# Latent attention in a hybrid trunk: scores from rounded and low parts, outputs by key tile

## The reference, cut to what matters

```python
q = (c_q @ w_uq).reshape(B, L, H, 192)            # 128 + 64 rotary
kv = (c_kv @ w_ukv).reshape(B, L, H, 128 + 128)   # keys, values
k = concatenate([kv[..., :128], k_pe shared by the heads])
q, k = rms_norm(q, g_q), rms_norm(k, g_k)         # then rotary on the last 64
s = einsum("bqhd,bkhd->bhqk", q, k) * scale       # where(mask, s, NEG_INF)
o = einsum("bhqk,bkhd->bqhd", softmax(s), v)
y = o.reshape(B, L, H * 128) @ w_o
```

## Time and profile before

| | us |
|---|---|
| median of 3 runs | 2914.8 |
| the three runs | 2919.31, 2914.8, 2913.06 |
| span of the profiled execution (PE busy 96% of it) | 2919.8 |
| the profiled execution's own time: highest of the runs, beside its span | 2919.31 |
| PE busy, of the span | 2817.5 |
| DVE, ACT, POOL busy | 1800.3, 926.7, 670.6 |
| mean granted clock of PE, as a share of 2.4 GHz | 0.983 |

### The profile page before, as it was taken

One profiled execution on the slowest core, in us unless ns is written; L12 is line 12 of the kernel. 1 busy time (PEld: TensorE's weight loads), 2 busy tenths in 40 slices (PEclk: granted clock), 3 DMA queues, 4 the chain that ended last, 5 costly groups with the idle time before them and its releaser, 6 DMA issues. The chain is left out here.

```text
span 2919.8 us, 57859 instructions
## 1 busy us (share of the span) xinstructions
PE 2817.5 (96%) x23164; PEld 2700.8 (93%) x23164; DVE 1800.3 (62%) x2735; ACT 926.7 (32%) x1407; POOL 670.6 (23%) x327
## 2 busy tenths in 40 slices
PE   8999999999999999999878999999999999999999
PEld 7788999998888899999768999999999999899987
DVE  5443677713777687778796687741354535787730
ACT  4443322222444232222264322222222223332221
POOL 2111100043322220003532400024433334200033
PEclk9998999999999999999889999999999999999999
DMA  3100222232211122232300222233322122122232
GB/s 131 44 23 30 80 93 88 99 101 92 66 61 58 36 95 88 92 95 86 104 2 24 95 80 93 91 104 101 108 79 95 61 91 75 44 94 92 87 115 80
DMA packets 65558, 231.53 MB, mean 79 GB/s; under 512 B 8048, under 2 KB 8816, under 8 KB 64912
## 3 DMA queue, kind: packets, MB, share of 16 engines
q1 hardware_dynamic: 62784, 222.56, 23.3%
q10 hardware_dynamic: 2640, 7.02, 0.7%
HBM read 227.45 MB, written 2.10 MB: 79 GB/s over the span
## 5 line engine op out<-in xcount | busy, mean ns | idle before, releaser
L238 PE MATMUL ps<-xs,wr 128*128 128x264 f32 x12864 | 1577.4, 284 | 17.5 <-POOL wr L216 9.9
L238 PEld LDWEIGHTS ps<-xs,wr 128*128 128x128 f32 x12864 | 1561.9, 188 | 24.2 <-POOL wr L216 9.9
L216 POOL TENSOR_TENSOR wr<-raw,wr 128x1024 fp32r<-128x1024 f32 x240 | 588.6, 2458 | 2073.3 <-ACT wr L208 2072.7
L238 PE MATMUL ps<-hid,wr 128*128 128x264 f32 x5376 | 657.6, 284 | 10.4 <-POOL wr L216 6.0
L238 PEld LDWEIGHTS ps<-hid,wr 128*128 128x128 f32 x5376 | 653.7, 189 | 12.5 <-POOL wr L216 6.6
L208 ACT ACTIVATE wr<-raw 128x1024 fp32r<-128x1024 f32 x416 | 434.2, 1048 | 345.8 <-PE ps L238 264.9
L466 DVE TENSOR_TENSOR ub<-ps,rstd 128x528 f32<-128x528 f32 x176 | 124.4, 707 | 145.7 <-PE ps L238 145.0
L216 DVE TENSOR_TENSOR wr<-raw,wr 128x1024 fp32r<-128x1024 f32 x176 | 214.2, 1217 | 0.0
L526 ACT ACTIVATE hid<-scr 128x528 f32 x88 | 56.8, 646 | 382.2 <-DVE scr L485 382.2
L523 ACT ACTIVATE scr<-scr 128x528 f32<-128x528 f32 x88 | 56.9, 646 | 368.1 <-DVE scr L481 368.1
L478 DVE SCALAR_TENSOR_TENSOR scr<-ub,convp,scr 128x528 f32<-128x528 f32 x176 | 135.3, 769 | 26.0 <-DVE scr L475 21.1
(11 more groups left out here) (295 smaller groups left out, 2328.0 us busy)
## 6 DMA issues: line engine op xcount, KB each, us to landing
raw<-in_stream SPq DMA_DIRECT2D x416, 512.0 KB, 3.7
work<-in_ret_tab ACTq DMA_DIRECT2D x4, 1056.0 KB, 5.3
h<-in_h SPq DMA_DIRECT2D x8, 264.0 KB, 6.4
out<-h SPq DMA_DIRECT2D x8, 256.0 KB, 4.3
work<-in_s_b ACTq DMA_DIRECT2D x1, 512.0 KB, 3.5
work<-in_s_c ACTq DMA_DIRECT2D x1, 512.0 KB, 5.4
convp<-in_convp ACTq DMA_DIRECT2D x4, 88.0 KB, 2.3
work<-in_mla_tab ACTq DMA_DIRECT2D x1, 264.0 KB, 2.6
```

The source lines that it names most:

```text
L216: pool.tensor_tensor(wr[:, s, 1].rearrange("p a b -> p (a b)"), raw[:, s, :], wr[:, s, 0].rearrange("p a b -> p (a b)").bitcast(F32), ALU. ...
L238: mm = pe.matmul(out[:, q], wr[:, slot, w, b0 + k], x[k][v][:, q * HALF:(q + 1) * HALF], start=start and k == 0 and p == 0, stop=stop and ...
```

## The change

Scores: `qn, qr, kn, kr` are each split into a rounded part (ACT, `part_high`) and a low part (DVE, `part_low`) in fp32r, one set for all heads, and a score tile is the sum of three products for each of the two key parts (high by high, high by low, low by high). The 528 keys of block 3 go as 264 and 264, in two banks, and the mask is one fp32r matmul of 64 columns per block. Outputs: instead of one for each query block, `output` runs once for each head, in the next head's cycle where O3 was, over all 512 queries: the meta values by 512 columns, then key tile t by the queries from block t on (512, 384, 256, 128 columns), still in fp32. For that `pt` holds all transposed blocks, and the meta keys are transposed first. The last head's outputs are made in two parts, OA (blocks 0 to 2) and OB (block 3). ACT's and DVE's splits of the outputs go from four of 128 columns to one of 512. The diff, without the semaphore lists and the tables of waits that go with it (the waits for outputs now name O, OA or OB), and without the SBUF addresses:

```diff
-            CYCLE = (("S0", 0), ("S1", 0), ("O3", -1), ("S2", 0), ("SPK", 1), ("SPQ", 1), ("T0", 0), ("S3", 0), ("kn", 2), ("qn", 2),
-                     ("qr", 2), ("T1", 0), ("O0", 0), ("T2", 0), ("O1", 0), ("O2", 0), ("SUM", 2), ("T3", 0))
+            CYCLE = (("S0", 0), ("S1", 0), ("O", -1), ("S2", 0), ("SPK", 1), ("SPQ", 1), ("T0", 0), ("S3", 0), ("kn", 2), ("qn", 2),
+                     ("qr", 2), ("T1", 0), ("T2", 0), ("SUM", 2), ("T3", 0))
...
+            FINAL = (("S0", 0), ("S1", 0), ("O", -1), ("S2", 0), ("T0", 0), ("S3", 0), ("T1", 0), ("T2", 0), ("TM", 0),
+                     ("OA", 0), ("OM", 0), ("out0", 0), ("T3", 0), ("out1", 0), ("OB", 0))
...
+                def products(out, q, k, stop):
+                    for s, t in (("qn", "kn"), ("qr", "kr")):
+                        for v, w in PRODUCTS:
+                            pe.matmul(out, parts[s][v][:, q], parts[t][w][:, k], start=s == "qn" and (v, w) == PRODUCTS[0],
+                                      stop=stop and s == "qr" and (v, w) == PRODUCTS[2])
...
                     if b == 0:
-                        pe.wait_ge(p_scaled.sem, p_scaled.done("qr", h))
-                        pe.matmul(f[0:META, K:K + META], qn[j][:, 0:META], kn[j][:, 0:META], start=True, stop=False)
-                        pe.matmul(f[0:META, K:K + META], qr[j][:, 0:META], kr[j][:, 0:META], start=False, stop=True)
-                    for c0, c1 in ((0, min(K, 512)), (512, K)):
-                        if c0 < c1:
-                            pe.matmul(f[:, c0:c1], qn[j][:, q0:q0 + P], kn[j][:, c0:c1], start=True, stop=False)
-                            pe.matmul(f[:, c0:c1], qr[j][:, q0:q0 + P], kr[j][:, c0:c1], start=False, stop=False)
-                    for c0, c1 in ((K - 64, min(K, 512)), (512, K)):
-                        if c0 < c1:
-                            mm = pe.matmul(f[:, c0:c1], hide, ones[0:1, 0:c1 - c0], start=False, stop=True)
+                        pe.wait_ge(p_lo.sem, p_lo.done("qr", h))
+                        products(f[0:META, K:K + META], slice(0, META), slice(0, META), True)
+                    s = scored(b, h)
+                    for c0, c1 in ((0, K),) if b < QB - 1 else ((0, HALF), (HALF, K)):
+                        products(s[:, c0:c1], slice(q0, q0 + P), slice(c0, c1), c1 < K)
+                    mm = pe.matmul(s[:, K - 64:K], hide, every[0:1, 0:64], start=False, stop=True)
                     mm.then_inc(a_pe.sem, a_pe.one(f"S{b}"))
...
+                def output(name, h, b0, b1):
+                    o = o_pe if name == "O" else e_pe
+                    free(name, h)
+                    f = line(name, h)
+                    pe.wait_ge(a_act.sem, a_act.done(f"copy{b1 - 1}", h))
                     d = slice(h * VDIM, (h + 1) * VDIM)
+                    pe.matmul(f[:, b0 * P:b1 * P], vt[0:META, QB, d], pt[0:META, 0, b0 * P:b1 * P], start=True, stop=False)
+                    for t in range(b1):
+                        q = slice(max(t, b0) * P, b1 * P)
+                        mm = pe.matmul(f[:, q], vt[:, t, d], pt[:, t + 1, q], start=False, stop=t == b1 - 1)
+                    mm.then_inc(o.sem, o.one(name))
...
+                def part_low(s, h):
+                    dve.wait_ge(p_hi.sem, p_hi.done(s, h))
+                    dve.tensor_tensor(parts[s][1], whole(s, h), parts[s][0].bitcast(F32), ALU.subtract)\
+                       .then_inc(p_lo.sem, p_lo.one(s))
...
                 mean_squares(1)
+                for s in ("kn", "kr", "qn", "qr"):
+                    part_low(s, 0)
                 for h in range(HEADS):
...
-                    low(0, h)
                     share(3, h)
+                    if not last:
+                        for s in ("kn", "kr", "qn", "qr"):
+                            part_low(s, h + 1)
                     if h + 2 < HEADS:
                         rot(h + 2)
...
+                def part_high(s, h):
+                    act.wait_ge(p_scaled.sem, p_scaled.done(s, h))
+                    if h and s == "kn":
+                        act.wait_ge(a_pe.sem, a_pe.done("S3", h - 1))
+                    one(p_hi, s, parts[s][0], whole(s, h), ACT.Copy)
...
                     rotary(h)
+                    if h == 1:
+                        for s in ("kn", "kr", "qn", "qr"):
+                            part_high(s, 0)
                     roots(h)
...
                     soft(3, h)
+                    if not last:
+                        for s in ("kn", "kr", "qn", "qr"):
+                            part_high(s, h + 1)
                     if more:
                         query(h + 2)
                         round_unit(act, uH + h + 2 + AHEAD)
                         rotary(h + 2)
                     copy(1, h)
-                    high_out(0, h)
                     copy(2, h)
```

More of the change, by code:

```diff
@@ L151, in trunk @@
         convp = sb("convp", [P, 2 * KT, 4])
+        every = sb("every", [P, 192], F32R)
         work_at = hid_at + 8 * 2 * T * 4
@@ L570, in mla @@
             flat_work = work[:].rearrange("p a b -> p (a b)")
-            parity = lambda k: [work[:, 4 * j + k] for j in range(2)]
-            qn, qr, kn, kr = (parity(k) for k in range(4))
+            parts = {s: [parts_[:, 2 * k + v] for v in range(2)] for k, s in enumerate(("qn", "qr", "kn", "kr"))}
             krot, sqkr, tab, misc = (work[:, k] for k in (8, 9, 10, 11))
@@ L578, in mla @@
             par, stat, joint = misc[:, 0:16], misc[:, 16:56], misc[:, 56:57]
-            hide = misc[0:1, 64:192]
+            hide = every[0:1, 64:192]
+            hidden = -2.0 ** 100
             small, total, inverse = misc[0:META, 192:200], misc[0:META, 200:208], misc[0:META, 208:216]
@@ L651, in mla @@
             NEW = ["x", "a", "b"]
-            l_dve = Order(sem("mla_l_dve"), ["hide", "show"] + [("kv", s) for s in NEW] + [("kv", "root")] + ["joint", "tab"] +
+            l_dve = Order(sem("mla_l_dve"), ["every", "hide", "show"] + [("kv", s) for s in NEW] + [("kv", "root")] + ["joint", "tab"] +
                           [("norm", 3), ("norm", 4), ("lo", 3), ("lo", 4)] + ["gain", "up", "down", "turned", "twice"] +
@@ L897, in last_cycle @@
                     out_part(1, h, range(HEADS - 1))
-                    output(3, h)
-                    pe.wait_ge(a_dve3.sem, a_dve3.done("lo3", h))
+                    output("OB", h, QB - 1, QB)
+                    pe.wait_ge(e_dve.sem, e_dve.done("OB"))
                     out_part(0, h, [HEADS - 1])
@@ L952, in dve_ @@
             def dve_(dve):
-                dve.memset(hide[:, 0:64], NEG).then_inc(l_dve.sem, l_dve.one("hide"))
-                dve.memset(hide[:, 64:P], 0.0).then_inc(l_dve.sem, l_dve.one("show"))
+                dve.memset(every[0:1, 0:64].bitcast(F32), 1.0).then_inc(l_dve.sem, l_dve.one("every"))
+                dve.memset(hide[:, 0:64].bitcast(F32), hidden).then_inc(l_dve.sem, l_dve.one("hide"))
+                dve.memset(hide[:, 64:P].bitcast(F32), 0.0).then_inc(l_dve.sem, l_dve.one("show"))
                 norm_dve(dve, n, g0)
@@ L1113, in dve_ @@
                     if h:
-                        low(3, h - 1)
+                        low("O", h - 1, 0, QB)
                     if not last:
@@ L1136, in dve_ @@
                         mean_squares(h + 2)
-                low(3, HEADS - 1)
-                dve.wait_ge(a_dve3.sem, a_dve3.done("lo3", HEADS - 1))
+                low("OB", HEADS - 1, QB - 1, QB)
+                dve.wait_ge(e_dve.sem, e_dve.done("OB"))
                 dve.sem_inc(tile_free, gO - gV)
```

121 lines of the change are left out of this document (55 added, 66 removed).

## The result

The changed kernel takes 2926.5 us (median of 20 runs, 2913.2 to 2929.8 without one run of 5502.6), the kernel before 2917.3 (20 runs, 2912.0 to 2924.4). The ratio is 1.002, with a 95% interval of 1.001 to 1.0029: slower by 0.1 to 0.3%. The profiled executions have spans of 2927.5 and 2919.8 us and mean granted clocks of 0.976 and 0.983. The forecast was 2921, 6.2 above the median of the three runs shown with it. The size was about right, and so was the kind of reason. Both halves of the sum were too small, as the stage shows.

What follows compares the result with a forecast made beforehand. PE, busy 96% of the span, was taken as the bound. Terms summed to -4.4 us at full clock and +6 for lower clock, +1.6 on the profiled 2919.8, so 2921.4; 2921 was chosen, range 2901 to 2930.

Steps and rivals of the forecast that it cites:

- Both halves of the sum: Whole kernel: -4.4 us at the full clock and +6 us from lower clock, together +1.6.
- The case called likeliest: Whole kernel: time as summed, 2921 us, own range 2915 to 2927; chance 0.5.
- the middle head: Heads 1 to 5: 22.9 us becomes 20.1 without waits, 21.7 with PE's 1.6 us wait.
- Scores: PE's score products S0 to S3: 7.3 us a head becomes 5.85, 1.5 less.
- The count by passes: Score tiles: three passes for four save a quarter of product time, some 0.25 us a head beyond the sum.
- Outputs: PE's output products: 4.46 us a head becomes 3.2, 1.3 less.
- ACT's queue: Four copies behind S3's exponential end ACT's chain at 8.4 us; PE, there at 6.8, waits 1.6.
- The clock: Half speed after idle stretches at the start (+5 us) and in heads 6 and 7 (+1): +6 us.
- fourth rival: Waits at the sums of squares cost clock in middle heads too: six stretches of 3.4 us, +10, 2931 us; chance 0.1.
- no stretch with PE idle for 3 us keeps the clock: Trace of the kernel before: no 3 us idle PE stretch keeps the clock; argued against the clock doing as before.
- The second: Rival for the whole kernel: clock does as before, -4.4 from the median, 2910 us (2907 to 2914); chance 0.23.
- The third: Rival: ACT's chain ends by PE's arrival, heads 0 to 5 gain another 1.6 us each; 2896 to 2906; chance 0.17.

Runs made afterwards that it cites:

- experiment 5: Changed kernel with 13 overwritten 512-column products filling PE's idle time ahead of head 0's first scores only: 2920.8 us, ratio 1.0015 to the kernel before.
- experiment 6: Changed kernel with ACT's rounding of a weight unit moved behind the square of the rotary part: 2910.3 us in one run.
- experiment 7: Changed kernel with the four rounding copies ahead of the key's operations and remaining PE waits filled with unread products: 2898.8 us, ratio 0.9935 to before.
- experiment 2: Kernel before with only the new outputs by key tile, scores left as they were: 2909.6 us, ratio 0.9963 to before.
- experiment 4: Changed kernel with ACT's four rounding copies ahead of the key's operations and DVE's subtractions ahead of the last share: 2911.7 us, ratio 0.9968 to before.
- experiment 10: Changed kernel with three more unread ACT copies of 264 columns among the part copies of heads 1 to 7: 2945.6 us, ratio 1.008 to before.
- experiment 3: Changed kernel with unread 512-column products in PE's waits at the start, sums of squares, T3 of head 6, S0 of head 7: 2912.4 us, ratio 0.9963.
- experiment 12: Kernel with early copies and filled waits, with the exponential of S3 moved ahead of the key's operations on ACT: 2899.3 us, ratio 0.9937 to before.
- experiment 11: Changed kernel with the idle time ahead of the first scores filled by 28 products of 128 columns: 2923.7 us, ratio 1.0017 to before.
- experiment 9: Kernel with early copies and filled waits, with two of four part copies moved back behind the exponential of S3: 2902.7 us, ratio 0.9949 to before.
- experiment 8: Kernel before with only the outputs changed, plus unread products filling PE's waits in heads 6 and 7: 2903.5 us, ratio 0.9955 to before.

## Why the prediction was right, and where not

**The total** came out 9.2 us above before in the medians (2926.5 against 2917.3) and 7.7 in the profiled spans, inside the range. The case called likeliest happened: a small gain in PE's work, and a larger loss to the clock. But the gain was put at 4.4 us and the clock at 6, and neither is right: they were 7.0 and 14.7. Like for like, profile against profile, the sum said +1.6 and the stage gave +7.7. The 2921 came out closer because it was chosen between the median of three runs and a profile 5 us above it, and because the two errors go against each other. That much of it is luck.

**At the full clock** the stage gained 7.0 us, not 4.4. First what half speed cost, as each window less that of the same head at the full clock: head 0 22.65 - 18.10 (experiment 5) = 4.6, head 3 25.97 - 21.23 = 4.7, head 5 0.2, head 6 21.12 - 16.57 (212.84 to 229.41 in experiment 6) = 4.6, head 7 40.37 - 30.33 (experiment 7) = 10.0, together 24.1. For before an estimate must do: one us at half speed cost 0.46 us in head 3 (4.74 in 10.4), so 20.5 cost 9.4. The difference is 14.7; the stage ended 7.7 later, so the rest is -7.0. By heads: the start +2.5 (first scores at 91.04 instead of 88.55; forecast +2.8); head 0 -3.2 (18.10 against 21.29, 88.55 to 109.84 before; forecast -2.9); heads 1 to 5 5 x (21.23 - 22.87) = -8.2 (forecast -6.0); head 6 +0.5 (16.57 against 18.26 - 0.46 x 4.7; forecast +0.7); head 7 +1.5 (30.33 against 37.68 - 1.56 - 7.3 = 28.8, its window in rows 1 ending 1.56 us after the last product starts; forecast +1.0). That adds to -6.9. The term that was mis-sized is the middle head: forecast 21.7, measured 21.23.

**Scores.** Forecast 1.35, 1.19, 1.53 and 1.78 us. The timeline gives 1.26, 1.08, 1.49 and 1.84, 5.67 instead of 5.85. S0 and S1 were 0.1 shorter each; the 0.2 us for one exposed load and drain was perhaps too much behind narrow records, but no run separates it. S0 got no faster than the 1.24 of before: the narrowest tile gains nothing, while S1 went from 1.48 to 1.08. The count by passes that the prediction took from the Trainium skill (FP8 and Floating Point Precision, TensorE Precision Notes) would have made S0's products a quarter shorter; S0 took 1.24 us before and 1.26 after, and the trace decides against it.

**Outputs.** Forecast 3.2 us, measured 3.21. The gain of 1.3 a head is confirmed by itself in experiment 2 (22.87 to 21.54 or 21.57).

**ACT's queue.** Forecast, counted from the first projection: key product at 1.78, copies from 3.65 to 5.9, the end of the square at 8.4, PE at the sums at 6.8, a wait of 1.6. Measured with the projection at 124.62: 1.76, 3.53 to 5.66, 8.3, 6.87, and 1.47. Experiment 6 takes one term out of this queue and gets its full length back, experiment 4 takes four out and the wait is gone, experiment 10 puts three in and the wait grows by 0.95. This step is shown. What the prediction did not ask is whether the copies could stand elsewhere: ACT was idle for 2.94 us right ahead of them.

**DVE** was forecast to be done with its subtractions 7.3 us after the first projection; they ended 6.8 after it, hidden as said.

**The clock** is the step that failed, and in one term. The start was put at 10 us of half speed and +5; it had 10.2 and cost 4.6. Heads 6 and 7 with their own waits were put at 22 us and +1; the two stretches behind those waits (from 244.9 and 261.9) had 23.9, and head 7's 10.0 less the 9.4 of before is +0.6. The waits at the sums of squares were put at nothing; in the profiled run two of the six were followed by 10.2 us each, and cost 4.7 + 0.2 + 4.6 = 9.5. The prediction knew this price only as its fourth rival, with 0.1. The reason named in the text (idle stretches cost the clock that follows) was right, and experiments 3, 5 and 7 show it: with its waits filled, the same kernel's last product starts at 269.60 instead of 286.26. For the 0.1 the text gives no row, and the trace of before had some, in another layer: behind PE waits of 1.51, 1.61 and 1.60 us (ending at 1498.8, 1514.6 and 1557.1, among shorter ones) the clock was at half speed for 6.8, 3.4 and 6.8 us, and behind one of 1.47 us amid wide products (1023.7) it held. That no stretch with PE idle for 3 us keeps the clock is true of that trace but for its first: PE waits 9.94 us for its first weights, and the clock is at 1.00 up to the first scores.

**The rivals.** The second (the clock does as before) is refuted. The third (ACT's chain ends in time) is refuted by the wait of 1.44 or 1.47 in every head, though experiment 4 shows what it would have brought. The fourth was given 0.1, as a case beside the first, and holds together with it: its losses came after two of six waits, at 10.2 us each instead of six of 3.4, and weigh 9.5 of the 14.7 us where it had said 10. Experiment 10 shows how they grow.

## What to carry to other kernels

Before a small operation is added to an engine that is a third busy, ask where in its queue it lands: four copies of 0.53 us hid almost completely one place earlier, and cost 1.5 us a head where they stood. On a kernel bound by TensorE, count each wait twice, once for itself and once for the clock: in the profiles 3.55 us of idling cost 4.6 more, and a wait of 1.44 us cost 4.7 more in two cases of six. Look where a low stretch begins, not only in which window it lies. Where a wait can't be removed, products that nobody reads, into a bank that is overwritten next, bought that back here (2912.4 us in experiment 3, against 2926.5). And of two changes made together, time each alone: one of these was worth -0.4% and the other +1.2%. The two don't add up to the +0.2% of both: the scores alone had two waits of 1.05 us a head, both together one of 1.44 or 1.47.

## What was not expected of the hardware

- The clock loss follows idle time, and filling the idle removes it, with products of 128 columns as well as 512 (head 0 18.08 and 18.10 us, against 22.65 unfilled). One profile of each kernel says so; the medians of those two runs (ratios 1.0015 and 1.0017, against 1.002 unfilled) are too near to confirm it.
- It is not idle time alone: in experiment 12 PE had no wait in head 4 or ahead of it, and 3.4 us at half speed came in the middle of wide products (171.6 to 175.0). The stretches of 3.4 us in middle heads of experiments 3, 4, 5, 6, 10 and 12 all begin in the output products, 3.4 to 3.6 us after the head's first scores, with waits at the sums ahead of them from 0 to 2.4 us. The stretches of 10.2 us behind the waits at the sums, in the changed kernel and in experiments 5, 10 and 11, all begin 0 to 1.3 us ahead of a head's first scores. In the kernel of experiment 7, no such stretch was seen. What sets the short ones off stays open.
- The same program differs by up to 16.6 us from run to run, and the granted clock follows: the four runs of the changed kernel with a mean clock of 0.982 have spans of 2911.4 to 2912.8 us, the four at 0.976 2927.5 to 2928.0. The profiled run is one of the latter, so its 54.8 us at half speed are more than the median run had; no trace shows which stretches the faster runs were spared. The five runs of experiment 7 lay within 3.7 us, but the nine of experiment 9, with the same waits filled, within 18.8, so that a narrower spread by filling is not shown.
- The starts of the first scores differ by 1 to 2 us between profiles for reasons outside the stage (91.11 and 92.16 in experiments 7 and 12, which are alike up to there; 88.63 and 87.09 in experiments 2 and 8). Differences of that size between single profiles are not to be read as an effect.
